# Products of zeros between the narrow score products of a gated linear attention scan

## The reference, cut to what matters

```python
def step(S, xs):
    qc, kc, vc, gc = xs
    b = jnp.cumsum(gc, axis=2)
    o_inter = jnp.einsum('bhck,bhkv->bhcv', qc * jnp.exp(b), S)
    diff = b[:, :, :, None, :] - b[:, :, None, :, :]
    decay = jnp.exp(jnp.where(causal, diff, -jnp.inf))
    a = jnp.einsum('bhik,bhjk,bhijk->bhij', qc, kc, decay)
    o = o_inter + jnp.einsum('bhij,bhjv->bhiv', a, vc)
    b_last = b[:, :, -1:, :]
    S_new = jnp.exp(b_last[:, :, 0, :, None]) * S + jnp.einsum('bhck,bhcv->bhkv', kc * jnp.exp(b_last - b), vc)
    return S_new, o
```

## Time and profile before

| what | value |
|---|---|
| time, median of 3 runs | 1815.48 us (1814.99 to 1817.98) |
| the profiled execution's own time | 1819.45 us |
| its span, first to last instruction | 1817.5 us |
| mean granted TensorE clock in it | 0.956 |
| PE busy | 1693.0 us, 93% of the span |
| DVE, ACT, POOL busy | 62%, 45%, 24% |
| chain that ended last, by engine | PE 74%, DVE 12%, ACT 8% |

### The profile page before, as it was taken

How to read it: one execution, slowest core, us unless ns; L and a number is a source line. 1 busy time by engine, 2 the same in 40 slices (tenths; PEclk the granted TensorE clock), 3 DMA queues, 4 the chain that set the end, 5 groups by cost and what they waited for, 6 DMA issues and landing times.

```text
span 1817.5 us, 33516 instructions
## 1 busy us (share of the span) xinstructions
PE 1693.0 (93%) x13615; PEld 1561.8 (86%) x13615; DVE 1125.9 (62%) x1718; ACT 826.0 (45%) x1371; POOL 442.7 (24%) x376
## 2 busy tenths in 40 slices
PE   7999988999999998999789898898988999999997
PEld 6989866999999997999788797676764999999997
DVE  6071366776767675476776764787723686757673
ACT  4253254452635352333455544676753352626261
POOL 4345225100000003445222221587922200000000
PEclk9999779999999999999999899799998999999999
DMA  4212122312313232331321210001285132222221
GB/s 178 93 48 93 50 99 96 140 53 88 140 47 138 75 114 97 112 122 47 117 105 47 93 59 1 1 2 48 78 340 233 51 123 106 94 93 92 92 92 47
DMA packets 26149, 170.15 MB, mean 94 GB/s; under 512 B 2154, under 2 KB 13978, under 8 KB 16234
## 3 DMA queue, kind: packets, MB, share of 16 engines
q1 hardware_dynamic: 23434, 133.31, 19.6%
q0 software_dynamic: 2592, 35.13, 5.2%
HBM read 156.26 MB, written 12.17 MB: 93 GB/s over the span
## 4 chain that ended last, share of the span: by engine, by line
PE 74%; DVE 12%; ACT 8%; issue 3%; POOL 1%; DMA 0%; ACTq 0%; DVEq 0%; SPq 0%; PEldq 0%
PE slot L2890 19%; PE slot L2655 16%; PE slot L2819 14%; PE slot L3007 3%; PE slot L2842 3%; PE slot L2738 2%; PE slot L2624 2%; ACT phase L1695 2%; PE slot L3015 2%; PE slot L2985 1%; PE slot L3145 1%; POOL phase L1070 1%; DVE xt_rest L2384 1%; PE slot L2699 1%; PE slot L3205 1%
## 5 line engine op out<-in xcount | busy, mean ns | idle before, releaser
L2819 PE MATMUL slot<-h_high,w_high 128*128 128x260 f32 x784 | 222.0, 283 | 1.7 <-DVE normed_x L2190 1.7
L2819 PE MATMUL slot<-h_high,w_rest 128*128 128x260 f32 x784 | 221.6, 283 | 0.0
L2819 PE MATMUL slot<-h_rest,w_high 128*128 128x260 f32 x784 | 221.3, 282 | 0.0
L2890 PE MATMUL slot<-u_high,w_high 128*128 128x260 f32 x1024 | 206.7, 283 | 0.0
L2890 PE MATMUL slot<-u_rest,w_high 128*128 128x260 f32 x1024 | 205.7, 282 | 0.0
L2890 PE MATMUL slot<-u_high,w_rest 128*128 128x260 f32 x1024 | 205.4, 282 | 0.0
L2890 PEld LDWEIGHTS slot<-u_high,w_rest 128*128 128x128 f32 x1024 | 157.9, 188 | 0.0
L2890 PEld LDWEIGHTS slot<-u_high,w_high 128*128 128x128 f32 x1024 | 157.4, 188 | 0.5
L2890 PEld LDWEIGHTS slot<-u_rest,w_high 128*128 128x128 f32 x1024 | 157.6, 188 | 0.0
L1070 POOL TENSOR_SCALAR phase<-phase 128x128 f32<-128x128 f32 (+3 forms) x128 | 140.8, 1116 | 47.5 <-DVE phase L1805 47.1
L1012 POOL TENSOR_TENSOR pw_rest<-weights,pw_high 128x1024 fp32r<-128x1024 f32 x18 | 43.4, 2410 | 442.7 <-ACT pw_high L1332 426.3
(11 more groups left out here) (455 smaller groups left out, 4614.7 us busy)
## 6 DMA issues: line engine op xcount, KB each, us to landing
weights<-in_wt SPq DMA_DIRECT2D x47, 2048.0 KB, 8.0
weights<-in_state SPq DMA_DIRECT2D x2, 2048.0 KB, 8.4
out<-weights SPq DMA_DIRECT2D x2, 2048.0 KB, 8.4
weights<-in_w SPq DMA_DIRECT2D x2, 2048.0 KB, 8.7
out<-phase SPq DMA_DIRECT2D x6, 512.0 KB
x_rows<-residual SPq DMA_DIRECT2D x1, 2080.0 KB, 6.7
residual<-x_rows SPq DMA_DIRECT2D x1, 2080.0 KB, 10.6
phase<-in_x_prompt SPq DMA_DIRECT2D x2, 1024.0 KB, 7.0
```

Source lines behind the costliest of these rows:

```text
L2819: last = mm(bank, weights[w][:, KH * half + k, :], h_part[m][:, of_h, k, :], start=start and k == 0 and w == 0 and m == 0, stop=k == KH - ...
L2890: last = mm(ps[:, a, 0:HT], w[:, k, :], m[:, k, HT * a:HT * a + HT], start=k == 0 and w is high and m is x_high, stop=k == DC - 1 and w is ...
```

## The change

After every second narrow product (for s = 0, 2, 4 and 6) the changed kernel issues one more product of the identity with zeros over the 512 columns of the bank that holds the scores. It adds zero to all of them, so the values stay what they were. That is 4 products in each chunk, 16 in each head's block and 64 in all, each with its own weight load of 128 columns. Nothing else changes: no semaphore, no buffer and no order.

```diff
                             last = mm(ps[0:w, 0, i0:i0 + SUB], kp2[:, h % 2, KOFF[s] + w * c:KOFF[s] + w * c + w],
                                       qp2[:, h % 2, i0:i0 + SUB], start=False, stop=c == TT - 1 and s == NSUB - 1,
                                       skip_group_check=True)
+                            if s % 2 == 0:
+                                mm(ps[:, 0, :], identb, zerosb, start=False, stop=False, skip_group_check=True)
                     last.then_inc(fu, 1)
```

## The result

The changed kernel takes 1837.23 us (median of 5 executions, 1826.37 to 1838.45) against 1817.98 us before on the same chip (1814.99 to 1820.84). The ratio is 1.0101, 95% interval 1.0078 to 1.0124: some 18 us more (14 to 23). Run once more beside other kernels it was at 1.0086 (1.0057 to 1.0115). So the change makes the kernel slower, inside the range of the prediction and 6 us under its likeliest case. The kernel before came out 2.5 us slower than in the three runs that the forecast starts from; change for change, 18 to 19 us stand against a forecast of 27.9.

The account below looks back on a forecast made before the run. PE's blocks of narrow score matmuls, mostly at half clock, were taken to be on the path. Heads 0, 2, 3 at +9.9, +8.9, +9.3 and head 1 at +3.7 less 3.9 gave 1815.5 + 27.9 = 1843 us, range 1821 to 1853.

Parts of the forecast that it names:

- likeliest case: Scan: blocks of heads 0, 2 and 3 at half clock, head 1's at full; +27.9 us, 1843 us, chance 0.38.
- The rests ahead of the blocks: PE's rests ahead of heads 0, 2 and 3 cost the clock as before; those blocks are entered and stay at half.
- The price of a product of zeros: In the blocks: 0.22 us at full, 0.43 at half, extra at width changes; a block 10.4 or 18.0 us.
- Fewer blocks at half: Scan: zeros hold the clock in head 0's block, so two blocks at half; +17.7, 1833 us, chance 0.24.
- The zeros bring the clock back inside a block: In blocks at half, the clock returns half way, 3.8 us less for three blocks; +8.5, 1824 us, chance 0.10.
- All stay at full: All four blocks at full: 1812 us at the estimated price, chance 0.07; 1804 us if zeros hide loads, 0.05.
- The term for what comes back: Work behind the blocks of heads 0 to 3 at full clock gives back 2.6, 3.9, 2.9 and 2.8, together 12.2 us.

Follow-up runs that it names:

- The filled rests: Changed kernel plus 10, 10 and 8 products of zeros in PE's rests ahead of the blocks of heads 0, 2 and 3; ratio 0.9982 to the kernel before.
- the first trace: Profiled execution of the changed kernel in its first measurement, against the kernel before; that execution 1830.22 us, median 1837.23 us, ratio 1.0101.
- the second trace: Profiled execution of the same changed kernel, run once more without further edits; ratio 1.0086 to the kernel before.
- the kernels with cheap zeros: Rests filled, zeros inside blocks only between wide weights (80 to 128 columns), three or two a chunk; ratios 0.9909 and 0.9900 to the kernel before.
- three cheap zeros: Rests filled, zeros inside blocks only after s = 4, 5 and 6 instead of 0, 2, 4 and 6; ratio 0.9909 to the kernel before.

## Why the prediction was right, point by point

**The rests ahead of the blocks** were the right cause. The blocks that the likeliest case names lost the clock, those of heads 0, 2 and 3; head 1's ran at full, and the time behind head 1 came back (3.6 us, forecast 3.9). The way there was right for head 0 alone: heads 2 and 3 were to be entered at half, but were entered at full and fell 1.0 and 0.7 us later. So a full clock at the entry is not enough behind a rest, and the zeros do not hold it there. The filled rests show the cause and don't only argue it: with the same zeros inside, the blocks went from half to full when the rests were filled, and 16 to 18 us above before became 3 under. In the four traces with filled rests and zeros inside, all 16 blocks are at 1.00; in the four with open rests none of the 12 blocks of heads 0, 2 and 3 is.

**The price of a product of zeros** was mis-sized for one kind. Beside narrow weights the forecast was 0.40 us at full and 0.69 at half, measured 0.42 and 0.66; the step from narrow to zeros, for which there was no row, takes 0.08 and 0.09 us in the starts of the first trace, against the 0.09 and 0.13 taken over from the step back. Between wide weights the forecast was 0.22 and 0.43, measured 0.14 and 0.27: the product of zeros hides a load of the product behind it (the one at 222.09), which I had allowed for as a bound only. A block at half became 16.4 us instead of 18.0, at full 9.94 instead of 10.4. For three blocks at half and one at full this is 3 x 1.6 + 0.5 = 5.3 of the 6.7 us by which the scan's +21.2 is under the forecast +27.9; most of the rest is that heads 2 and 3 ran their first microsecond at full. The rule of the Trainium skill (TensorE: Matmul & The Clock Gate, "Step-by-step: what each phase is for"), that the next weights load while a product runs, agrees with the loads at 213.43 and 222.09 and not with the one at 223.51: it holds here from narrow to narrow and from wide to wide.

**The rivals.** "Fewer blocks at half", 1833 us, is the second trace: head 0's block at full for the most part, and the scan 14.7 us longer where this rival had 17.7. That its execution took 1834.30 us is luck; the first trace, with three blocks at half, took 1830.22. So the two cases with the largest chances, 0.38 and 0.24, are both what this kernel does, from one execution to the next, and its median of 1837.23 lies between their 1843 and 1833. "The zeros bring the clock back inside a block" happened in head 0's block of the second trace, early, but not in that of the first nor in head 2's of the second, which were also entered at half. The reading it was held against, that the clock came back in unbroken long products only, was too narrow already for the kernel before: in head 1's block it came back about 1 us in, among narrow products (0.82 from 212 to 214 us, 1.00 from 214 to 216). "All stay at full" never happened by itself. It needs the filled rests, and with them its time was 3 us under before, as its 1812 said. That is luck: the blocks were cheaper (39.8 us, not 41.6), but only 6.7 us came back (forecast 12.2), and the traced scan gained nothing.

**The term for what comes back**, 12.2 us if every block holds the clock, was near the 11.4 and 10.6 of the kernels with cheap zeros, but not head by head. Behind head 2's block it was too high: 0.4 us of 2.9 came back with three cheap zeros (11.75 us from that block to head 3's, 12.11 before). There I named no engine that would be late next; it is DVE, and then ACT. Behind head 3's block 4.3 us came back, where 2.8 were forecast.

## What to carry to other kernels

Look for where the clock is lost before padding what runs slowly: products of zeros belong into the rests of PE ahead of a stretch of narrow products, where they cost nothing, and inside the stretch only as many as hold the clock. Put them between products whose weights are as wide as theirs; between narrow ones a wide product cost two and a half to three times as much here. And when such padding is weighed, price it at half clock too: at the lower level the padding itself was 1.6 to 1.9 times as dear, so it makes slower exactly what it was meant to speed up.

## What the runs showed of the hardware that was not expected

A product of zeros of 512 columns between wide fp32 weights adds 0.14 us at full clock to a row of narrow products, less than the 0.22 us it takes alone, because a load of the product behind it runs under it. The same zeros at their neighbours' width (16 to 112 columns) add (2.07 - 1.35) / 4 = 0.18 us on average, with narrow neighbours too. The late load is not a matter of zeros: in the kernel before, two fp32 products of 64 and 80 columns start 0.14 us apart at full clock, of 32 and 48 columns 0.11, but of 80 and 96 columns 0.07 and of 48 and 64 columns 0.05.

The same program is granted the clock in different places from one execution to the next: head 0's block took 16.40 us in one trace of the changed kernel and 10.54 in another, and a stretch of the sparse attention, which nobody touched, cut at the same two products, 241.00 us at a clock of 0.95 in the first of them and 248.20 at 0.91 in the second. What decides this was not tried.
